# One-column products of the first feed-forward weights, spread between the steps of the output projection's last tile

## The chip, the cores and the metric

One Trainium2 chip, one of its cores. The metric is the device time of one execution in microseconds (us); lower is better. A core has five engines that run their own instruction streams and wait for each other through semaphores: TensorE (PE; its weight loads are shown apart as PEld), VectorE (DVE), ScalarE (ACT), GpSimd (POOL) and SyncE (SP), which issues most of the transfers.

## What is computed

Two transformer blocks run one after the other on 512 tokens of width 1024. The part that matters here is the end of the first block's token mixer and the start of its feed-forward network:

```python
x = x + g1 * token_mixer(...)                    # its last step: merged @ w_out
x = x + g2 * conv_ffn(ada_norm(x, norm2_g, sh2, sc2), p)

def ada_norm(x, g, shift, scale):
    return rmsnorm(x, g) * (1 + scale) + shift

def conv_ffn(h, p):
    u, g = jnp.split(h @ p['ffn_w_up'], 2, axis=-1)
    ...
```

The norm's input to `ffn_w_up` is a scaled x, divided by the root of a token's mean square, plus a shift that is the same for every token. So `h @ w` can be had from the raw, not yet divided x: (raw x @ w) / root + shift @ w. The kernel does this for the first pair of feed-forward tiles, and therefore needs `shift @ w` for those 2 x 128 columns: these are the one-column products that the change moves.

## The kernel before, in words

**Layout and precision.** Activations lie transposed: 128 channels on the partitions, eight tiles of channels, 512 tokens along the free axis. Each weight matrix comes in chunks of (mostly) 8 x 256 columns. SyncE loads a chunk into one of three staging buffers (WS), ScalarE writes its high part (WH, `hi_chunk`, line 88) and VectorE the rest (WL, `lo_chunk`, line 92). A product of a chunk with an activation is three matmuls per channel tile: high x high, high x low, low x high (`prod`, lines 477 to 479), so a tile of 128 outputs x 512 tokens takes 8 steps (k) of 3 matmuls. `prod_by_rows` (lines 498 to 500) does two output tiles at once, one channel tile after the other, and waits for each channel tile as it becomes ready.

**The output projection** (`out1_pe`) has 4 chunks and 8 output tiles n. Tile 7 is computed in PSUM bank 7; tile 6 in bank 0. VectorE (`out1_dve`) adds tile n to x (key "out1", n), sums squares and makes the low part of the raw scaled x; ScalarE squares and makes its high part. At the head of each chunk i both engines first convert a later chunk (OUT1+i+1, for i = 3 this is UP1, the first chunk of the feed-forward network).

**In the last tile**, TensorE runs six of the eight steps, then `shifted_pe`: for two groups of 128 columns, eight matmuls of 128 x 128 staged weights (float32, straight from WS) with one column of the shift, into bank 0, columns 0 and 1. Before them it waits for the low part of chunk UP1 and for VectorE having read bank 0 ("out1", 6). The last one signals "shifted". Then come the sums of seven squares over the channels (`seven_pe`, line 508), and then the last two steps of the tile. A float32 matmul shows in the trace as two passes, so the 16 products are 32 records of line 1602, and the four matmuls of line 508 are 8 records.

**Who waits for what.** SyncE waits for "shifted" before it loads chunk UP1+3 into the staging buffer of UP1 (line 397). VectorE waits for it before it copies the two columns out of bank 0 (line 1647), after the norm's diagonal. `up_pe` starts right behind `out1_pe` with the raw product of chunk UP1 (`prod_by_rows`); after two of its steps it adds the eighth square's sums (`eighth_pe`), from which ScalarE and VectorE get the norm; chunk UP1+1 then needs the normed x, and chunk UP1+2 is converted by VectorE after the last normed tile.

**Where to look:** the call is at line 1584 in `out1_pe`, `shifted_pe` at lines 1595 to 1604, `seven_pe` above line 508, the waits of the other engines at lines 397 and 1647. `modv_pe` (line 1419), two float32 matmuls with one column each, is a like piece of work in the same part of the kernel. The order on each engine is the order of the code; there is no scheduler.

Of the kernel before, what the change touches and what calls it, by code (L numbers as in the profile page):

```python
# [13 lines left out]
L = 512  # L14
# [117 lines left out]
def build(nc, A, out):  # L132
# [8 lines left out]
    def bank(b, n=512, p0=0, p1=128, off=0):  # L141
        return PS[p0:p1, b * 512 + off:b * 512 + off + n]

    pe, dve, acts, pool = (Tally(nc.alloc_semaphore(n)) for n in ("pe_done", "dve_done", "act_done", "pool_done"))
# [166 lines left out]
    def modcol(part, k, j=0):  # L311
        return MT[:, 8 * part + k, j:j + 1]
# [28 lines left out]
    UP1 = len(chunks)  # L341
# [31 lines left out]
    def stage(j):  # L373
        nk, n = chunks[j][1:3]
        return WS[:, slot(j), 0:nk * n]

    def weights(j):
        nk, n = chunks[j][1:3]
        return tuple(w[:, place(j), 0:nk * n].rearrange("p (k n) -> p k n", k=nk) for w in (WH, WL))
# [86 lines left out]
    def terms(w, wl, c, n=128, tok=(0, L), XX=(XHT, XLT), nk=8, k0=0):  # L466
        return [(w[:, k, c:c + n], wl[:, k, c:c + n], XX[0][:, k0 + k, tok[0]:tok[1]],
                 XX[1][:, k0 + k, tok[0]:tok[1]]) for k in range(nk)]
# [4 lines left out]
    def prod(e, o, trms, key=None, first=True, last=True):  # L473

        n = len(trms)
        for i, (lh, ll, rh, rl) in enumerate(trms):
            e.matmul(o, lh, rh, start=first and i == 0, stop=False)  # L477
            e.matmul(o, lh, rl, start=False, stop=False)  # L478
            ins = e.matmul(o, ll, rh, start=False, stop=last and i == n - 1)  # L479
        if key:  # L480
            ins.then_inc(*pe.to(*key))
# [7 lines left out]
    def prod_by_rows(e, outs, trms, ready, key, between={}):  # L489


        for k in range(8):
            if k in between:
                between[k]()
            e.wait_ge(*ready(k))
            for o, tm in zip(outs, trms):
                lh, ll, rh, rl = tm[k]
                e.matmul(o, lh, rh, start=k == 0, stop=False)  # L498
                e.matmul(o, lh, rl, start=False, stop=False)  # L499
                ins = e.matmul(o, ll, rh, start=False, stop=k == 7)  # L500
        ins.then_inc(*pe.to(*key))
# [3 lines left out]
    def sums_pe(e, name, tile, n, start, stop, key, step=512):  # L505
        for i, x in enumerate(range(0, n, 128)):
            w = min(128, n - x)
            ins = e.matmul(bank(3, 1, p1=w, off=step * i), tile[:, x:x + w], ONE[:, 0:1], start=start, stop=stop)
        ins.then_inc(*pe.to(*key))

    def spread_pe(e, name, n):

        e.wait_ge(*dve.at(name, "diagonal"))
        w = min(128, n)
        e.matmul(bank(3, n), ONE[0:w, :], RST[0:w, 0:n], start=True, stop=True).then_inc(*pe.to(name, "spread"))
# [4 lines left out]
    def seven_pe(e, name, n):  # L520
        e.wait_ge(*dve.at(name, "sum", 6))
        sums_pe(e, name, T[2], n, True, False, (name, "sums", 6))
# [893 lines left out]
    def modv_pe(e, i):  # L1416
        e.wait_ge(*dve.at("mod_half", i, 1))
        for m in range(2):
            ins = e.matmul(bank(7, 1, off=m), MACC[:, 128 * m:128 * m + 128], ONE[:, 0:1], start=True, stop=True)
        ins.then_inc(*pe.to("mod_sum", i))  # L1420
# [139 lines left out]
    def out1_bank(n):  # L1560
        return bank((1, 7, 2, 0, 1, 2, 0, 7)[n])

    def out1_pe(e):
        for i in range(4):
            j = OUT1 + i
            w, wl = weights(j)
            e.wait_ge(*dve.at("wl", j))
            tm = [terms(w, wl, 128 * m, XX=(MGH, MGL)) for m in range(2)]
            if i == 0:
                e.wait_ge(*dve.at("branch", 57))  # L1570
                prod_by_rows(e, [out1_bank(0), out1_bank(1)], tm, lambda k: dve.at("mg_lo", k), ("out1", 1))
            else:
                for m in range(2):
                    n = 2 * i + m
                    if n < 4:
                        e.wait_ge(*dve.at("branch", 56 + n if n == 2 else 63))
                    else:
                        e.wait_ge(*dve.at("out1", n - 3 if n > 4 else 1))
                    if n < 7:
                        prod(e, out1_bank(n), tm[m], ("out1", n))  # L1580
                    else:
                        e.wait_ge(*dve.at("mod", 23))
                        prod(e, out1_bank(n), tm[m][:6], last=False)
                        shifted_pe(e)
                        seven_pe(e, "norm2", L)
                        prod(e, out1_bank(n), tm[m][6:], ("out1", n), first=False)
            pe.name("w", j)
            if i == 2:
                e.wait_ge(*dve.at("meta_rms"))
            if i == 1:  # L1590
                spread_pe(e, "meta", 16)
                e.wait_ge(*dve.at("out1", 1))
                modv_pe(e, 23)

    def shifted_pe(e):

        e.wait_ge(*dve.at("wl", UP1))
        e.wait_ge(*dve.at("out1", 6))
        w = stage(UP1).rearrange("p (k n) -> p k n", k=8)
        for m in range(2):  # L1600
            for k in range(8):
                ins = e.matmul(bank(0, 1, off=m), w[:, k, 128 * m:128 * m + 128], modcol(3, k), start=k == 0,
                               stop=k == 7)
        ins.then_inc(*pe.to("shifted"))

    def out1_act(a):
        for i in range(4):
# [976 lines left out]
    def tensor(e):  # L2584
        front_pe(e)
        proj_pe(e)
        mix_pe(e)
        na_pe(e)
        gate_pe(e)
        out1_pe(e)  # L2590
        up_pe(e, "up1", UP1, "norm2", True)
        down_pe(e, "down1", "up1", DN1)
        foxp_pe(e)
        fox_pe(e)
        out2_pe(e)
        up_pe(e, "up2", UP2, "norm4", False)
        down_pe(e, "down2", "up2", DN2, "norm5")
        mean_pe(e, "norm5", L)
# [274 lines left out]
```

## Time and profile before

| | |
|---|---|
| median of 3 runs | 1680.36 us |
| lowest, highest | 1675.89 us, 1681.28 us |
| the profiled execution: span, first to last instruction | 1680.7 us |
| the profiled execution's own time outside the span | not given |
| TensorE busy | 1640.0 us, 98% |
| VectorE busy | 919.1 us, 55% |
| ScalarE busy | 632.4 us, 38% |
| mean granted TensorE clock | 0.988 of full |

All durations come from the one profiled execution. The ends of matmuls are modelled and overlap the next ones, so for TensorE the starts are read, not the durations: consecutive starts of 512-column matmuls lie 0.22 to 0.23 us apart.

### The profile page before, as it was taken

What the parts mean: (1) busy time and instruction counts of PE and PEld (TensorE: products, weight loads), DVE (VectorE), ACT (ScalarE), POOL (GpSimd) and SP (SyncE); (2) the same over time, 40 slices, a digit from 0 to 9 for tenths busy, and PEclk for the clock granted to TensorE, in tenths of its full rate; (3) what the DMA queues carried; (4) which work ended last, traced back from release to release, by engine and by line L of the source; (5) the groups of instructions that cost most, each with busy time, mean ns of one, the idle gap of its engine ahead of it and who ended that gap; (6) DMA issues with size and microseconds to landing.
All of it is one profiled execution on the core that took longest, in us unless ns stands there. A gap on an engine that the chain in (4) does not pass through costs nothing.

```text
span 1680.7 us, 20208 instructions
## 1 busy us (share of the span) xinstructions
PE 1640.0 (98%) x7941; PEld 1333.0 (79%) x7941; DVE 919.1 (55%) x1262; ACT 632.4 (38%) x816; POOL 92.6 (6%) x130
## 2 busy tenths in 40 slices
PE   8999999999999999999999999999999999999997
PEld 3588777878887888888888789977768888888885
DVE  5665686677667654444444574145766544444323
ACT  2352458432233343333332533146653332223221
POOL 0100000111010000000000100003420000000000
PEclk9899999999999999999999999999999999999998
DMA  9432101755444233332234221224442333332331
GB/s 320 129 119 80 44 26 51 226 164 179 160 150 151 64 102 85 101 101 77 86 103 131 86 76 52 76 65 96 97 127 75 101 100 101 100 90 66 92 104 51
DMA packets 227365, 176.71 MB, mean 105 GB/s; under 512 B 15812, under 2 KB 213316, under 8 KB 227270
## 3 DMA queue, kind: packets, MB, share of 16 engines
q1 hardware_dynamic: 220662, 151.23, 30.9%
q0 software_dynamic: 6608, 24.19, 4.4%
q8 instruction: 63, 1.03, 0.3%
q14 instruction: 32, 0.26, 0.0%
HBM read 166.84 MB, written 2.13 MB: 101 GB/s over the span
## 4 chain that ended last, share of the span: by engine, by line
PE 83%; DVE 9%; ACT 4%; issue 1%; SPq 1%; DMA 1%; DVEq 0%; POOLq 0%; POOL 0%; ACTq 0%
PE PS L477 23%; PE PS L479 23%; PE PS L478 23%; PE PS L2393 2%; PE PS L486 1%; DVE WL L92 1%; DVE T L92 1%; DMA MODW<-in_w_mod 1%; PE PS L498 1%; PE PS L500 1%; PE PS L499 1%; SPq L2682 1%; PE PS L649 1%; ACT WH L88 1%; DVE SUMS L111 1%
## 5 line engine op out<-in xcount | busy, mean ns | idle before, releaser
L477 PE MATMUL PS<-XH,WH 128*128 128x512 f32 (+2 forms) x1264 | 481.1, 381 | 3.2 <-DVE WL L92 1.1
L478 PE MATMUL PS<-XL,WH 128*128 128x512 f32 (+2 forms) x1264 | 476.8, 377 | 0.0
L479 PE MATMUL PS<-XH,WL 128*128 128x512 f32 (+2 forms) x1264 | 476.8, 377 | 0.0
L92 DVE TENSOR_TENSOR WL<-WS,WH 128x2048 fp32r<-128x2048 f32 (+3 forms) x131 | 272.8, 2083 | 209.4 <-ACT WH L88 206.6
L477 PEld LDWEIGHTS PS<-XH,WH 128*128 128x128 f32 (+1 forms) x1264 | 236.0, 187 | 48.9 <-DVE WL L92 2.0
L479 PEld LDWEIGHTS PS<-XH,WL 128*128 128x128 f32 (+1 forms) x1264 | 235.9, 187 | 44.8
L478 PEld LDWEIGHTS PS<-XL,WH 128*128 128x128 f32 (+1 forms) x1264 | 236.0, 187 | 43.2 <-issue 0.7
L88 ACT ACTIVATE WH<-WS 128x2048 fp32r<-128x2048 f32 (+3 forms) x131 | 229.1, 1749 | 76.2 <-PE PS L479 46.7
L477 PE MATMUL PS<-HH,WH 128*128 128x512 f32 x352 | 137.2, 390 | 0.2 <-DVE WL L92 0.2
L478 PE MATMUL PS<-HL,WH 128*128 128x512 f32 x352 | 136.9, 389 | 0.0
L479 PE MATMUL PS<-HH,WL 128*128 128x512 f32 x352 | 136.9, 389 | 0.0
L88 ACT ACTIVATE T<-T 128x512 f32<-128x512 f32 x45 | 28.5, 632 | 172.4 <-DVE T L92 138.8
L477 PEld LDWEIGHTS PS<-HH,WH 128*128 128x128 f32 x352 | 66.1, 188 | 14.3 <-DVE WL L92 0.6
L478 PEld LDWEIGHTS PS<-HL,WH 128*128 128x128 f32 x352 | 66.1, 188 | 13.8
L479 PEld LDWEIGHTS PS<-HH,WL 128*128 128x128 f32 x352 | 66.1, 188 | 13.6
L92 DVE TENSOR_TENSOR T<-PS,RST 128x512 f32<-128x512 f32 x47 | 32.5, 692 | 78.3 <-PE PS L479 69.2
L103 DVE SCALAR_TENSOR_TENSOR T<-PS,VT,T 128x511 f32<-128x511 f32 x42 | 31.5, 750 | 54.7 <-ACT T L88 53.9
L88 ACT ACTIVATE T<-X 128x512 f32<-128x512 f32 x40 | 25.3, 632 | 90.4 <-DVE X L92 58.9
L103 DVE SCALAR_TENSOR_TENSOR MACC<-MSRC,CACT,MACC 128x256 f32<-128x256 f32 x112 | 54.3, 485 | 8.3 <-DMA MSRC<-in_w_mod 3.6
L477 PE MATMUL PS<-WH,XH 128*128 128x256 f32 (+1 forms) x192 | 54.4, 283 | 0.0
L478 PE MATMUL PS<-WL,XH 128*128 128x256 f32 (+1 forms) x192 | 53.8, 280 | 0.0
L479 PE MATMUL PS<-WH,XL 128*128 128x256 f32 (+1 forms) x192 | 53.7, 280 | 0.0
(373 smaller groups left out, 2294.7 us busy)
## 6 DMA issues: line engine op xcount, KB each, us to landing
WS<-in_w_in SPq DMA_DIRECT2D x24, 1024.0 KB, 5.4
WS<-in_ffn_w_up SPq DMA_DIRECT2D x44, 512.0 KB, 4.9
WS<-in_ffn_w_in SPq DMA_DIRECT2D x44, 512.0 KB, 4.8
MSRC<-in_w_mod POOLq DMA_DIRECT2D x32, 512.0 KB, 4.9
WS<-in_fox_w_in SPq DMA_DIRECT2D x16, 1024.0 KB, 5.6
WS<-in_ffn_w_down SPq DMA_DIRECT2D x16, 704.0 KB, 4.5
WS<-in_ffn_w_out SPq DMA_DIRECT2D x16, 704.0 KB, 4.5
MODW<-in_w_mod SPq DMA_DIRECT2D x8, 1024.0 KB, 11.7
```

Source lines behind the costliest of these rows:

```text
L88: self.e.activation(o, i, f, scale=scale, **kw).then_inc(*self.done.to(*key))
L92: self.e.tensor_tensor(o, a, b, op).then_inc(*self.done.to(*key))
L103: self.e.scalar_tensor_tensor(o, a, s, b, op0, op1).then_inc(*self.done.to(*key))
L111: self.e.reciprocal(o, a).then_inc(*self.done.to(*key))
L477: e.matmul(o, lh, rh, start=first and i == 0, stop=False)
L478: e.matmul(o, lh, rl, start=False, stop=False)
L479: ins = e.matmul(o, ll, rh, start=False, stop=last and i == n - 1)
L486: ins = e.matmul(o, l, r, start=i == 0, stop=i == n - 1)
L498: e.matmul(o, lh, rh, start=k == 0, stop=False)
L499: e.matmul(o, lh, rl, start=False, stop=False)
L500: ins = e.matmul(o, ll, rh, start=False, stop=k == 7)
L2393: ins = e.matmul(PS[:, b + q0:b + L], VP[h % 2][0:k, t, :], P[h % 2][0:k, PFROM[t]:PFROM[t] + L - q0], start=t == 0, stop=t == 4)
```

## The change

The last tile's eight steps are run one by one. After each of the steps 1 to 6, TensorE computes 3, 3, 2, 3, 3 and 2 of the 16 one-column products (6, 6, 4, 6, 6 and 4 passes); after step 6 come the sums of seven squares, then step 7. The waits for the low part of UP1 and for "out1", 6 stand before the first one-column product, so after step 1 instead of after step 5. The products themselves, their banks and their results are the same.

```diff
--- before.py
+++ after.py
@@ -1580,10 +1580,13 @@
                         prod(e, out1_bank(n), tm[m], ("out1", n))
                     else:
                         e.wait_ge(*dve.at("mod", 23))
-                        prod(e, out1_bank(n), tm[m][:6], last=False)
-                        shifted_pe(e)
-                        seven_pe(e, "norm2", L)
-                        prod(e, out1_bank(n), tm[m][6:], ("out1", n), first=False)
+                        for k in range(8):
+                            prod(e, out1_bank(n), tm[m][k:k + 1], ("out1", n) if k == 7 else None, first=k == 0, last=k == 7)
+                            if 1 <= k < 7:
+                                for p in range(*((0, 3), (3, 6), (6, 8), (8, 11), (11, 14), (14, 16))[k - 1]):
+                                    shifted_pe(e, *divmod(p, 8))
+                            if k == 6:
+                                seven_pe(e, "norm2", L)
             pe.name("w", j)
             if i == 2:
                 e.wait_ge(*dve.at("meta_rms"))
@@ -1592,16 +1595,15 @@
                 e.wait_ge(*dve.at("out1", 1))
                 modv_pe(e, 23)
 
-    def shifted_pe(e):
-
-        e.wait_ge(*dve.at("wl", UP1))
-        e.wait_ge(*dve.at("out1", 6))
+    def shifted_pe(e, m, k):
+
+        if m + k == 0:
+            e.wait_ge(*dve.at("wl", UP1))
+            e.wait_ge(*dve.at("out1", 6))
         w = stage(UP1).rearrange("p (k n) -> p k n", k=8)
-        for m in range(2):
-            for k in range(8):
-                ins = e.matmul(bank(0, 1, off=m), w[:, k, 128 * m:128 * m + 128], modcol(3, k), start=k == 0,
-                               stop=k == 7)
-        ins.then_inc(*pe.to("shifted"))
+        ins = e.matmul(bank(0, 1, off=m), w[:, k, 128 * m:128 * m + 128], modcol(3, k), start=k == 0, stop=k == 7)
+        if m + k == 8:
+            ins.then_inc(*pe.to("shifted"))
 
     def out1_act(a):
         for i in range(4):
```

## Rows read from the trace of the kernel before

**Rows 1.** The page: span, and TensorE's busy time.

```profile
span 1680.7 us, 20208 instructions
...
PE 1640.0 (98%) x7941; PEld 1333.0 (79%) x7941; DVE 919.1 (55%) x1262; ACT 632.4 (38%) x816; POOL 92.6 (6%) x130
```

**Rows 2.** The page: chain that ended last, shares by engine and line.

```profile
PE PS L477 23%; PE PS L479 23%; PE PS L478 23%; PE PS L2393 2%; PE PS L486 1%; DVE WL L92 1%; DVE T L92 1%; DMA MODW<-in_w_mod 1%; PE PS L498 1%; PE PS L500 1%; PE PS L499 1%; SPq L2682 1%; PE PS L649 1%; ACT WH L88 1%; DVE SUMS L111 1%
```

**Rows 3.** Busy time by stretch: engines, PEclk the granted clock, DMA.

```profile
core 0: us, PE busy (x) PEld busy (x) DVE busy (x) ACT busy (x) POOL busy (x), PEclk, DMA share, GB/s
...
550.00:554.00 4.00, 4.00 (x32) 3.73 (x30) 1.44 (x2) 1.55 (x3) 0.00 (x0) 0.98 0.00 0
554.00:557.60 3.60, 3.60 (x18) 3.60 (x19) 0.00 (x0) 0.00 (x0) 0.00 (x0) 0.50 0.05 13
...
560.70:564.00 3.30, 3.30 (x20) 2.83 (x18) 1.35 (x2) 1.36 (x2) 0.00 (x0) 1.00 0.05 11
```

**Rows 4.** Timeline of TensorE: start us, us, engine line op out<-in xcount.

```profile
548.72 0.39 PE L477 MATMUL PS<-MGH,WH 128*128 128x512 f32 x1
...
551.44 4.59 PE L1602 MATMUL PS<-MODT,WS 128*128 128x1 f32 x32
555.89 1.84 PE L508 MATMUL PS<-ONE,T 128*128 128x1 f32 x8
557.60 0.77 PE L477 MATMUL PS<-MGH,WH 128*128 128x512 f32 x1
...
560.30 0.58 PE L498 MATMUL PS<-GXH,WH 128*128 128x512 f32 x1
560.72 0.39 PE L499 MATMUL PS<-GXL,WH 128*128 128x512 f32 x1
```

**Rows 5.** Chain of waits in order of time: start us, us, what.

```profile
563.39 0.80 PE PS L508 x8
...
564.59 1.93 ACT WH L88
...
582.63 2.30 DVE WL L92
...
584.98 0.50 PE PS L477
```

**Rows 6.** Timeline of VectorE, end of the output projection.

```profile
546.81 2.29 DVE L92 TENSOR_TENSOR WL<-WS,WH 128x2048 fp32r<-128x2048 f32 x1 [1.24 <-ACT WH L88]
549.21 0.75 DVE L103 SCALAR_TENSOR_TENSOR X<-PS,MODT,X 128x512 f32<-128x512 f32 x1
550.65 0.69 DVE L92 TENSOR_TENSOR T<-T,T 128x512 f32<-128x512 f32 x1 [0.70 <-ACT T L88]
```

**Rows 7.** Timeline of TensorE, eight one-column passes at full clock.

```profile
563.23 0.95 PE L508 MATMUL PS<-ONE,T 128*128 128x1 f32 x8
564.04 0.49 PE L498 MATMUL PS<-GXH,WH 128*128 128x512 f32 x1
564.36 0.40 PE L499 MATMUL PS<-GXL,WH 128*128 128x512 f32 x1
```

**Rows 8.** Timeline, VectorE and TensorE: four one-column passes behind a wait.

```profile
529.74 0.75 DVE L103 SCALAR_TENSOR_TENSOR X<-PS,MODT,X 128x512 f32<-128x512 f32 x1
...
530.46 0.61 PE L1419 MATMUL PS<-ONE,MACC 128*128 128x1 f32 x4
...
530.93 0.48 PE L477 MATMUL PS<-MGH,WH 128*128 128x512 f32 x1
```

**Rows 9.** Timeline of ScalarE: high part of chunk UP1+3.

```profile
587.28 1.92 ACT L88 ACTIVATE WH<-WS 128x2048 fp32r<-128x2048 f32 x1
```

**Rows 10.** Busy time by stretch elsewhere, columns as in rows 3.

```profile
203.00:207.00 4.00, 1.66 (x9) 1.10 (x8) 3.13 (x5) 3.75 (x4) 0.00 (x0) 1.00 0.00 0
...
1192.00:1195.60 3.60, 2.01 (x9) 1.24 (x8) 3.26 (x5) 0.59 (x1) 0.62 (x2) 1.00 0.89 204
1195.60:1199.00 3.40, 3.40 (x18) 3.20 (x16) 2.82 (x7) 0.00 (x0) 0.00 (x0) 0.50 0.29 75
```

## The prediction

> **What bounds the kernel now.** I read the page's head first: TensorE is busy for 98% of the span [rows 1], and the chain that ended last runs through its lines [rows 2]. So a change of TensorE's order counts wherever the chain is on TensorE, and other engines count only where they make it wait. Next, the granted clock by stretch around the edited call. In 550 to 554 it is 0.98, in 554 to 557.6 it is 0.50, and from 560.7 on it is 1.00 again [rows 3]: the two levels are 2.4 and 1.2 GHz. What TensorE did before the fall is in its timeline: from 551.44 it had only the 32 passes of line 1602, one column each, behind a stretch of 512-column matmuls [rows 4]. It was never idle there (busy 4.00 of 4.00) [rows 3], yet it came down to the half clock, and the rest of the passes, the sums and the last six matmuls ran at it.
>
> The chain then shows what hangs on the end of this tile: the last sums at 563.39, ScalarE's weights at 564.59, VectorE's normed tiles and weights up to 582.63, and TensorE again at 584.98 [rows 5]. All of it starts from the end of tile 7, so what this tile gains or loses passes on whole to 584.98 and, TensorE being the bound behind it, to the end.
>
> **The sum, step by step.** It is a difference of starts in one execution. That execution's span is 1680.7 us [rows 1]; what lies around the span is not given, and the median of the three runs is 0.3 us under the span, so I carry the difference to the median, 1680.36.
>
> *Price of a pass at full clock.* Eight passes behind a 512-column matmul start at 563.23, the next matmul at 564.04 and the one after it at 564.36 [rows 7]. Ordinary matmuls lie 0.227 apart: twelve between 548.72 and 551.44 take 2.72 [rows 4]. So the group costs 0.81, and 0.32 - 0.23 = 0.09 for the return to long matmuls, 0.90 together. Four passes that stood behind a wait take 530.46 to 530.93, 0.47 [rows 8], with the same 0.09 0.56; here the first weight load has nothing to hide behind. If that load costs as much as a pass, 8 passes are 0.90 and 5 are 0.56: 0.113 each, and a boundary costs nothing beyond it.
>
> *Removed: the half clock.* At full clock the 40 passes and six matmuls from 551.44 would take 40 x 0.113 + 6 x 0.227 = 5.88 and end at 557.32. The feed-forward product starts at 560.30 instead, and its first matmul takes 0.42 (to 560.72) where 0.23 is normal [rows 4]. That is 2.98 + 0.19 = 3.17 us lost. If the clock holds with the passes spread, all of it comes back: **-3.17**.
>
> *Added: a wait that was hidden.* "out1", 6 and the low part of UP1 are now awaited after step 1. Step 2 starts at 548.72 [rows 4], which is where the first pass would go. VectorE finishes the low part at 546.81 + 2.29 = 549.10 and only then runs the addition of tile 6, 549.21 + 0.75 = 549.96 [rows 6]. Neither moves: both follow ScalarE's conversion and tile 6, which are ahead of the edit. In a like wait TensorE started 0.03 before VectorE's recorded end, 530.46 against 529.74 + 0.75 = 530.49 [rows 8], so it goes on at 549.93. That is 1.21 of idle, and 0.11 for the weight load that now hides behind nothing: **+1.32**. Before, this wait was over long before 551.44. Its bounds are 0 (if VectorE is early) and 1.5. Behind the waiting product stand all further matmuls of the tile, and no other engine needs any of them before the tile's end.
>
> *Five more boundaries.* The passes stand in six groups instead of one (the last with the sums). By the equations above a boundary is worth 0. The bounds are one weight load of 0.11 gained or lost at each of five, -0.6 and +0.6; I take 0, because rows 7 is exactly such a group, hidden load, exposed return and all.
> The Trainium skill, TensorE: Matmul & The Clock Gate, Part 2 (Step-by-step), says that the queue pulls a weight load ahead of running matmuls. By that alone the spread would hide five more loads, 0.6 us, for 1677.9; the row shows that the matmul behind the group pays it back [rows 7].
>
> *Moved at no cost.* The sums of seven squares wait for 550.65 + 0.69 = 551.34 [rows 6] and now start near 557, so they don't wait. "shifted" comes near 557.0 instead of 555.9: the load of chunk UP1+3 is queued behind it on SyncE, about 1 us later, and ScalarE wants that chunk only at 587.28 [rows 9]. VectorE copies the two columns only after the norm's diagonal, which follows the sums at 563.39 [rows 5]. POOL has nothing here. If the first of these covers went, a late chunk would stop TensorE at its fourth pair of tiles, but 25 us lie between.
>
> Sum: -3.17 + 1.32 + 0 = -1.85. The feed-forward product should start at 548.72 + 1.32 + 40 x 0.113 + 6 x 0.68 = 558.64 instead of 560.30. 1680.36 - 1.85 = **1678.5 us**, 0.11% less. About 0.3%, here 5.0 us, is what a measurement of this kernel can tell from no change; the whole forecast lies inside it.
>
> **The rivals.**
>
> *The clock falls all the same (slower than before).* Place: the first group. The new wait leaves TensorE idle for 1.2 us, and the groups behind it are still half one-column passes. For it: two other falls have idle time just ahead, 2.01 busy of 3.60 before the 0.50 at 1195.6 [rows 10]. Against it: 1.66 busy of 4.00 at 203 to 207 left the clock at 1.00 [rows 10], and between the new groups stand 0.68 us of full matmuls. Before, there was nothing of the kind from 551.44 to the fall, which a mean of 0.98 over 550 to 554 [rows 3] puts near 553.85. Price: with the same 3.17 lost, only the wait is left, +1.32, 1681.7. It decides for slower as soon as the clock is down for more than 1.85 / 0.5 = 3.7 us; at half clock through all of the 8.6 us of work it would be 8.6 + 1.3 - 3.2 = +6.7, 1687.1.
> The Trainium skill, TensorE: Matmul & The Clock Gate, Part 1 (HAM oscillation), warns of long idle gaps between bursts of matmuls, and the same part says that the gate goes by how busy TensorE has been. Taken at its word it speaks against this change, which adds a gap and removes none; its time would be this rival's 1681.7. The trace disagrees in part: TensorE was busy without a gap and lost its clock [rows 3].
>
> *No wait shows.* If VectorE's order gives bank 0 earlier than the rows say, the whole 3.17 comes back: 1677.2. Against it stand two VectorE instructions in a row that end at 549.96 [rows 6].
>
> *It changes nothing to be seen.* If the fall of the clock comes in only some executions, or a later fall (the one at 1195.6 lasts 3.40 us [rows 10], which cost 1.7) comes or goes as everything shifts by 2 us, the difference may be nothing, 1680.4, or 1678.5 - 1.7 = 1676.8. For it: the three runs lie 5.4 us apart, more than the whole sum. Against it: the passes that brought the fall stand in the code and are the same in every execution.
>
> **How the numbers follow.** Forecast 0.60. Clock falls all the same 0.15, nearly all of it within 5 us of before. No wait shows 0.08. Nothing to be seen, or a later fall moved, 0.17. The range reaches down to 1675.0 (1676.8, and below it the 1.8 us that two medians of such runs may well differ by) and up to 1682.0, past the rival's 1681.7; up to 2 in 10 lie outside. Faster by over 0.3% needs 1675.3 or less: 0.10, from the last case's low end. Slower by over 0.3% needs 1685.4: 0.03, from a long half clock. Within: 0.87.
>
> **What would show it.** In the new profile: PEclk 1.00 from 548 to 564 (the rival: 0.50 somewhere in it); a gap in TensorE's timeline of about 1.2 us from 548.7, ended by VectorE's X; groups of 6, 6, 4, 6, 6 and 12 passes at 0.11 each with three matmuls between them; the first matmul of line 498 near 558.6; the last part of the chain before the feed-forward tiles (584.98 before) near 583.1; the chunk UP1+3 on time. The forecast is wrong if the clock is at half in that stretch, if the gap is missing or twice as long, or if the stretch gains its 1.85 us and the total doesn't.

## The result, and the profile after

The change made the kernel slower: a median of 1687.3 us over 22 runs (1674.7 to 1692.1) against 1680.7 over 22 runs of the kernel before (1675.6 to 1687.8), a ratio of 1.0033 with a 95% interval of [1.0018, 1.0048]. The forecast was 1678.5.

The two profiled executions hide this: their spans are 1680.4 us after and 1680.7 before. What tells them apart is the granted clock. By stretch, in the kernel after (columns: stretch, its length, busy time of PE, PEld, DVE, ACT, POOL with instruction counts, PEclk, DMA share, GB/s):

```profile
541.60:545.50 3.90, 2.67 (x15) 2.04 (x15) 3.10 (x3) 1.20 (x2) 0.00 (x0) 1.00 0.00 0
545.50:558.30 12.80, 12.80 (x49) 11.45 (x48) 0.88 (x2) 0.36 (x2) 0.00 (x0) 0.50 0.01 4
558.30:562.60 4.30, 4.30 (x11) 3.43 (x12) 1.19 (x2) 1.35 (x2) 0.00 (x0) 0.50 0.84 232
562.60:566.00 3.40, 3.40 (x20) 2.94 (x20) 1.12 (x3) 1.09 (x2) 0.00 (x0) 1.00 0.00 0
48.70:62.40 13.70, 12.48 (x29) 4.93 (x28) 11.80 (x19) 7.34 (x10) 3.37 (x3) 1.00 0.02 5
```

The clock falls at 545.5, 1.1 us behind the first of the moved passes (544.38), and stays at 1.2 GHz for 17.1 us, until 562.6. Before, the fall near the tile lasted from about 553.9 to 560.7, 6.8 us [rows 3]. The last row is luck, since the code there is the same in both kernels: in this execution the clock was full from 48.7 to 62.4, whereas in that of the kernel before it was at half (with the first matmul of its tile 7):

```profile
48.70:62.40 13.70, 12.87 (x15) 4.76 (x16) 8.61 (x14) 5.52 (x7) 3.36 (x3) 0.50 0.02 7
...
547.36 0.39 PE L477 MATMUL PS<-MGH,WH 128*128 128x512 f32 x1
```

So tile 7 begins at 541.64 instead of 547.36, 5.7 us earlier, before the change has done anything, and the change then gives it all back. TensorE's timeline after shows how:

```profile
542.77 0.39 PE L479 MATMUL PS<-MGH,WL 128*128 128x512 f32 x1
544.38 0.80 PE L1604 MATMUL PS<-MODT,WS 128*128 128x1 f32 x6 [1.23 <-DVE X L103]
545.05 0.48 PE L477 MATMUL PS<-MGH,WH 128*128 128x512 f32 x1
...
546.07 1.27 PE L1604 MATMUL PS<-MODT,WS 128*128 128x1 f32 x6
547.21 0.77 PE L477 MATMUL PS<-MGH,WH 128*128 128x512 f32 x1
...
555.89 0.85 PE L1604 MATMUL PS<-MODT,WS 128*128 128x1 f32 x4
556.59 1.85 PE L508 MATMUL PS<-ONE,T 128*128 128x1 f32 x8
558.30 0.77 PE L477 MATMUL PS<-MGH,WH 128*128 128x512 f32 x1
...
559.73 0.63 PE L498 MATMUL PS<-GXH,WH 128*128 128x512 f32 x1
```

Between the last matmul of step 1 and the first pass lie 1.61 us where 0.23 is normal: 1.38 of idle, ended by VectorE's addition of tile 6. The first group of six passes takes 0.67 (544.38 to 545.05), the second 1.14 (546.07 to 547.21), and a step of three long matmuls 1.42 instead of 0.68. From the start of tile 7 to the feed-forward product (line 498) it takes 559.73 - 541.64 = 18.09 us, before 560.30 - 547.36 = 12.94. The clock is back only at 562.6, after 4.3 us of long matmuls without passes. The long fall is probably not in every execution: two of the 22 took 1674.7 and 1674.9 us with a mean clock of 0.993, which is about 23 us at half clock in all, where the profiled one had 36. No trace of those two shows it.

Behind this the chain is as before and only later, so the loss passes on whole (chain of waits after; the answers of [rows 5]):

```profile
563.98 0.80 PE PS L508 x8
...
565.18 1.93 ACT WH L88
...
583.20 2.30 DVE WL L92
...
585.55 0.50 PE PS L477
```

From the start of tile 7 to here it is 43.9 us after and 37.6 before. The chunk UP1+3 was on time (ScalarE's timeline after, [rows 9]):

```profile
587.85 1.92 ACT L88 ACTIVATE WH<-WS 128x2048 fp32r<-128x2048 f32 x1
```

One execution of the experiment e4 below took 2728 us at a mean granted clock of 0.555; it was slow as a whole and is left out of e4's figures.

### The profile page after: what moved, and what is told of

The parts are those of the page before. It is cut to its first block, busy times and chain, and to the rows that moved or that the text cites. A ratio compares the mean times of both kernels' runs of the same rounds, so it can differ in the third digit from the quotient of the medians.

```text
span 1680.4 us, 20208 instructions
## 1 busy us (share of the span) xinstructions
PE 1639.0 (98%) x7941; PEld 1333.5 (79%) x7941; DVE 917.4 (55%) x1262; ACT 632.4 (38%) x816; POOL 92.3 (5%) x130
## 4 chain that ended last, share of the span: by engine, by line
PE 81%; DVE 11%; ACT 4%; issue 2%; DMA 1%; DVEq 0%; SPq 0%; POOLq 0%; POOL 0%; ACTq 0%
PE PS L477 23%; PE PS L479 23%; PE PS L478 22%; PE PS L2395 2%; DVE WL L92 2%; PE PS L486 1%; DVE T L92 1%; PE PS L614 1%; ACT WH L88 1%; PE PS L498 1%; PE PS L500 1%; PE PS L499 1%; DVE SUMS L111 1%; ACT NTP L88 1%; ACT T L88 1%
## 5 line engine op out<-in xcount | busy, mean ns | idle before, releaser
L92 DVE TENSOR_TENSOR T<-PS,RST 128x512 f32<-128x512 f32 x47 | 32.5, 691 | 78.3 <-PE PS L479 69.2
```

The source lines that it names most:

```text
L92: self.e.tensor_tensor(o, a, b, op).then_inc(*self.done.to(*key))
```

## The experiments

Two parts can be told apart: the wait that was moved ahead (idle time), and the spread of the passes. The first theory was that the spread mix brings the clock down and holds it down; its rival was that the idle time does. Both were wrong, and a third, that it takes the two together, was stated for the second set. All kernels below were timed in 12 runs each (e4 counts 11), beside the kernel before (29 to 35 runs, medians 1679.6, 1679.9 and 1680.1).

"Half clock" in the table is the time at half clock per execution, 2 x (1 - mean granted clock) x span, averaged over the runs; the clock of each run is given to 0.001, so a single run is good to 1.7 us only. The runs of one kernel scatter by about 10 us in it, so a mean of 12 runs is good to about 3 us. "At the tile" is the granted clock of the profiled execution from the start of tile 7 to the feed-forward product.

| kernel | median us | ratio to before, 95% | half clock, us | at the tile |
|---|---|---|---|---|
| before | 1679.6 to 1680.1 | 1 | 35.0, 36.6, 39.4 | 0.75 |
| the change, 22 runs | 1687.3 | 1.0033 [1.0018, 1.0048] | 49.7 | 0.61 |
| f1, the change again | 1686.6 | 1.0044 [1.0026, 1.0061] | 49.4 | 0.61 |
| e1, wait alone | 1679.7 | 1.0003 [0.9982, 1.0024] | 32.5 | 0.95 |
| e2, spread, no wait | 1676.1 | 0.9983 [0.9961, 1.0004] | 27.9 | 1.00 |
| f3, as e2, wait put back | 1685.3 | 1.0028 [1.0009, 1.0047] | 45.2 | 0.61 |
| f2, spread late | 1672.9 | 0.9973 [0.9953, 0.9993] | 24.6 | 1.00 |
| g2, f2 again | 1675.2 | 0.9965 [0.9943, 0.9987] | 27.4 | 1.00 |
| f4, wait early, spread late | 1678.4 | 0.9996 [0.9980, 1.0012] | 31.6 | 0.94 |
| g1, wait, then all together | 1683.4 | 1.0016 [0.9996, 1.0035] | 38.4 | 0.77 |
| g3, the change, half the products | 1675.7 | 0.9976 [0.9955, 0.9997] | 30.4 | 1.00 |
| e3, one or two a step, tiles 6 and 7 | 1675.8 | 0.9971 [0.9954, 0.9987] | 25.1 | 1.00 |
| e4, 15 of 16 products left out | 1676.6 | 0.9977 [0.9957, 0.9996] | 36.2 | 1.00 |

### e1: the wait alone

```diff
...
-                        prod(e, out1_bank(n), tm[m][:6], last=False)
+                        prod(e, out1_bank(n), tm[m][:2], last=False)
+                        e.wait_ge(*dve.at("wl", UP1))
+                        e.wait_ge(*dve.at("out1", 6))
+                        prod(e, out1_bank(n), tm[m][2:6], first=False, last=False)
                         shifted_pe(e)
```

> The 16 products stay together behind step 5 as before; only the two waits stand behind step 1. Theory 'mix' (short passes spread between long matmuls bring the clock down and keep it down; the wait is only its own idle time): at most the wait's 1.3 us over the kernel before, so a median of 1680 to 1684 and half clock of 3 to 10 us around the last tile. Theory 'wait' (the idle time ahead of the passes makes the clock fall and the rest follows): as slow as the change, 1685 to 1690, with half clock for over 10 us in that stretch.

```profile
541.60:553.60 12.00, 10.79 (x66) 9.26 (x66) 3.97 (x4) 1.56 (x3) 0.00 (x0) 0.95 0.12 33
552.50:555.90 3.40, 3.40 (x10) 2.65 (x9) 0.75 (x1) 1.25 (x2) 0.00 (x0) 0.50 0.98 276
```

No loss that can be measured, 1679.7. The same 1.2 us of idle is there (10.79 busy of 12.00), and the clock did not fall behind it. It fell only at 552.5, 0.9 us into the long matmuls behind the passes and the sums (they start at 551.59), and for 3.4 us, where the kernel before lost it in the middle of the passes and for 6.8. That does not make the wait free: over the runs there are 2.5 us less at half clock (32.5 against 35.0), within the scatter, and that much would be worth 1.25 of its 1.5 us. The theory that the idle time alone brings the loss is out.

### e2: the spread without the wait

```diff
-            e.wait_ge(*dve.at("wl", UP1))
-            e.wait_ge(*dve.at("out1", 6))
+            e.wait_ge(*acts.at("wh", UP1))
...
-        ins = e.matmul(bank(0, 1, off=m), w[:, k, 128 * m:128 * m + 128], ...
+        ins = e.matmul(bank(6, 1, off=8 + m), w[:, k, 128 * m:128 * m + 128], ...
...
```

> The change's order, but the products go to two free columns of bank 6 and wait only for ScalarE's high part of the chunk, so that no idle time stands behind step 1. Theory 'mix': the clock falls as with the change and stays at half until the dense matmuls are back, 1684 to 1690, about 1.3 us under the change. Theory 'wait': clock 1.00 through the tile, 1677 to 1680, under the kernel before.

```profile
542.30:552.30 10.00, 10.00 (x66) 8.99 (x65) 3.92 (x4) 1.56 (x3) 0.00 (x0) 1.00 0.02 3
```

1676.1, not over 1684: the mix of passes and long matmuls alone held the full clock, though half of the time of a step is passes (six at 0.113 beside three long matmuls at 0.227). It is also a little under the 1677 to 1680 of the other theory; the interval of its ratio touches 1. The theory that the mix brings the clock down by itself is out too. The tile took 10.00 us; the forecast's price list (24 matmuls of 0.227 and 40 passes of 0.113) gives 9.97.

### e3: a thinner mix over two tiles

Bank 6 as in e2; one product behind each step of tile 6 and 2, 1, 2, 1, 1, 1 behind steps 0 to 5 of tile 7, waiting only for the chunk to arrive:

```diff
+            e.wait_ge(ws_in[slot(UP1)], arrived[UP1])
...
+                    elif n == 6:
+                        for k in range(8):
+                            prod(e, out1_bank(n), tm[m][k:k + 1], ("out1", n) if k == 7 else None, first=k == 0, last=k == 7)
+                            shifted_pe(e, 0, k)
...
```

> One or two products (2 or 4 passes) a step, over tiles 6 and 7, into bank 6, waiting only for the chunk's arrival; no idle time, and the short passes are a quarter of TensorE's time where the change has a half. Theory 'mix': a thin mix holds the clock, so it stays at 1.00 but for a possible fall at the sums, 1676 to 1680. Theory 'wait': the same, 1677 to 1680; a rival that any one-column pass lets the clock fall gives over 1684.

```profile
537.90:551.80 13.90, 13.90 (x81) 12.10 (x80) 5.93 (x6) 4.62 (x6) 0.00 (x0) 1.00 0.13 34
```

The stretch shown begins in step 2 of tile 6. 1675.8, below before with its whole interval and as good as e2. Both theories had said very nearly this (1676 or 1677 to 1680), so it parted nothing.

### e4: 15 of the 16 products left out

```diff
-        for m in range(2):
-            for k in range(8):
+        for m in range(1, 2):
+            for k in range(7, 8):
...
```

> The kernel before with only the last of the 16 one-column products left, the other 15 left out, so the feed-forward network's first pair lacks its shift. If the loss of the kernel before is the 30 passes (3.4 us at full clock) and their half clock (3.2 us), this is 4 to 7 us under before, 1674 to 1677, with no half clock at the tile, though the falls early in the program stay. It bounds what any placement of the products can reach: before minus 3.2 us.

```profile
551.10:557.60 6.50, 6.50 (x35) 5.58 (x34) 3.91 (x4) 1.56 (x3) 0.00 (x0) 1.00 0.12 33
```

1676.6, at the edge of what was expected. In its profile the tile went through in 6.6 us at full clock, but in the mean over its runs the kernel spent 36.2 us at half clock, no less than before (35.0). The missing 30 passes are 3.4 us, and the means over the runs differ by 3.5 (1675.8 against 1679.3), so nothing of the half clock's 3.2 is seen back. Whether the clock fell elsewhere in those runs or at the tile after all isn't shown. So the bound that it was meant to give is blurred, and it came out no faster than kernels that do all the products.

### f1: the change again

> The change itself, measured again beside the others. The wait alone gave 1679.7 us against 1679.6 for before, the spread alone 1676.1. If the loss is real and comes from the two together: 1684 to 1690 again, and a stretch of over 10 us at half clock around the last tile. If the first measurement was an odd set of executions: 1676 to 1681, between the two single edits, and no such stretch.

```profile
545.90:563.90 18.00, 16.76 (x66) 14.59 (x64) 3.92 (x4) 1.56 (x3) 0.00 (x0) 0.61 0.09 25
563.90:566.90 3.00, 3.00 (x9) 2.32 (x8) 1.31 (x2) 1.35 (x2) 0.00 (x0) 0.50 0.71 199
```

The loss is real, 1686.6, and the tile again takes 18.0 us with the clock down to 566.9.

### f2 and g2: the spread, late enough that nothing waits

```diff
-                            if 1 <= k < 7:
-                                for p in range(*((0, 3), (3, 6), (6, 8), (8, 11), (11, 14), (14, 16))[k - 1]):
+                            if 3 <= k < 7:
+                                for p in range(4 * k - 12, 4 * k - 8):
```

> Bank 0 and the change's two waits, but the products come behind steps 3 to 6, four at a time, when both waits are over, so no idle time. Theory 'together' (idle time right ahead of the thin mix lets the clock fall, and the mix, at half clock, keeps it down): clock mostly 1.00, 1675 to 1679, like the spread without a wait. Theory 'groups' (larger groups are what hurts; eight passes a step are more than half the time): 1683 or more.

```profile
541.60:551.70 10.10, 10.10 (x65) 8.89 (x64) 3.98 (x4) 1.55 (x3) 0.00 (x0) 1.00 0.02 5
```

The bank and the waits of the change, only without idle time, and the kernel is faster than before, and under the 1675 to 1679 expected. Groups of eight passes, more than half of each step's time, don't hurt. Measured a second time:

> The best kernel so far, again: products behind steps 3 to 6, four at a time, bank 0, the change's waits. 1672.9 was measured, against 1676.1 for the spread behind steps 1 to 6 without a wait. If the gain over the kernel before is real, 1671 to 1677 and a ratio below 1 with its whole interval.

```profile
545.70:555.80 10.10, 10.10 (x66) 8.92 (x65) 3.95 (x4) 1.56 (x3) 0.00 (x0) 1.00 0.01 3
```

Again below before with its whole interval: 0.9965 [0.9943, 0.9987]. This is the change as it should have been placed, 1672.9 and 1675.2 us. Not all of the 6.9 and 4.8 us between the medians is shown to be the tile's doing: 12.94 to 10.08 us there, and 0.19 behind it, give 3.1. The time at half clock is 12 us less than before in both sets (24.6 against 36.6, 27.4 against 39.4) where the fall at the tile is 6.8 us; part of that can be scatter.

### f3: e2 with the wait put back

e2's bank 6, but the two waits of the change in place of the one on ScalarE.

> The change with the products in bank 6 and both of its waits kept: it differs from the spread without a wait (1676.1) by the idle time alone. Theory 'together': as slow as the change, 1684 to 1690. Theory 'bank' (bank 0 was what made the difference): 1677 to 1679, the 1.3 us of idle over the spread without a wait.

```profile
541.60:559.80 18.20, 16.97 (x66) 14.71 (x65) 3.97 (x4) 1.55 (x3) 0.00 (x0) 0.61 0.09 26
```

One edit, the idle time, moves e2's 1676.1 to 1685.3 and e2's 10.0 us of tile to 18.1. The two were timed in different sets, but their ratios to the kernel before, timed beside each, have intervals that lie apart (to 1.0004, and from 1.0009). The bank has no part in it.

### f4: the idle time early, the spread late

The waits stand behind step 1 as in the change, the products behind steps 3 to 6 as in f2.

> The idle time stays behind step 1, but two full steps (1.4 us of long matmuls) stand between it and the first products, which come four at a time behind steps 3 to 6. Theory 'together', strictly (idle and mix have to touch): 1677 to 1681. If it is enough that both fall in the same few us, it stays slow, 1683 to 1690.

```profile
542.20:554.30 12.10, 10.87 (x65) 9.38 (x64) 3.97 (x4) 1.56 (x3) 0.00 (x0) 0.94 0.06 15
```

1678.4: the long fall is avoided. The clock did fall in this profile, but only at 552.9, where the sums end, and for 3.4 us. f4 differs from the change in two things, the two dense steps (long matmuls without passes) between the idle time and the passes, and the grouping by eight; since the same groups alone are harmless (f2), the distance is the likelier reason, but no run has the change's own groups at that distance.

### g1: the wait, then all products at once

```diff
...
-                        prod(e, out1_bank(n), tm[m][:6], last=False)
+                        prod(e, out1_bank(n), tm[m][:2], last=False)
                         shifted_pe(e)
+                        prod(e, out1_bank(n), tm[m][2:6], first=False, last=False)
...
```

> Both waits behind step 1 as in the change, but all 16 products follow at once (32 passes), and steps 2 to 5 come dense behind them. The change has three things: idle time, the passes right behind it, and then 9 us in which passes and long matmuls alternate. If the alternation is what keeps the clock at half once it has fallen: it falls here too but is back within the dense steps, 3 to 10 us at half clock, 1679 to 1684. If idle time and passes touching is what costs, however they are arranged afterwards: over 10 us at half clock, 1684 to 1690.

```profile
541.70:546.10 4.40, 3.17 (x22) 2.58 (x21) 3.50 (x4) 1.55 (x3) 0.00 (x0) 1.00 0.00 0
546.10:552.90 6.80, 6.80 (x26) 6.22 (x26) 0.49 (x1) 0.00 (x0) 0.00 (x0) 0.50 0.22 59
552.90:556.40 3.50, 3.50 (x21) 2.99 (x21) 0.00 (x0) 0.00 (x0) 0.00 (x0) 1.00 0.68 185
```

The idle time and the passes touch here as in the change, and the clock falls near the same place, 1.6 us behind the first pass (1.1 in the change). But the long matmuls behind them are dense, starting at 549.88:

```profile
544.49 5.53 PE L1603 MATMUL PS<-MODT,WS 128*128 128x1 f32 x32 [1.23 <-DVE X L103]
549.88 0.77 PE L477 MATMUL PS<-MGH,WH 128*128 128x512 f32 x1
```

and 3.0 us later, at 552.9, the clock is back: 6.8 us at half instead of 17.1. The median, 1683.4, lies between before and the change; its interval still touches 1, so the size of its loss is not settled. Over the runs the time at half clock is that of the kernel before (38.4 against 39.4 us), and the means over the runs, 1682.2 against 1680.6, differ by no more than the wait.

### g3: the change with half of the products

Channel tiles 0 to 3 are left out of the shift's products, so 2, 1, 1, 2, 1 and 1 products stand behind steps 1 to 6, and the wait and its idle time are the change's.

> The change with half of the products left out (channel tiles 0 to 3), so the shift is summed over half of its channels: 1 or 2 products a step behind steps 1 to 6, the waits behind step 1 as in the change. If the share of one-column passes behind the idle time decides, a quarter instead of a half lets the clock stay or come back soon: 1675 to 1680, under 10 us at half clock. If any alternation holds it down: 1682 or more, 15 us or more at half clock.

```profile
541.80:551.50 9.70, 8.47 (x49) 7.12 (x49) 3.99 (x4) 1.56 (x3) 0.00 (x0) 1.00 0.03 7
```

With half of the passes behind the same idle time the clock held in the profile, the tile took 9.68 us, and the runs are below before with their whole interval (1675.7 us). So it is not any mix behind idle time that brings the long fall; how thick it has to be isn't shown. This also gives the price of the wait at full clock: 24 matmuls and 24 passes by the price list are 8.16, so the wait costs 1.52.

## Why the prediction was wrong

**The step that failed** is "If the clock holds with the passes spread, all of it comes back: -3.17". It didn't hold. At full clock the tile with its wait would take e2's 10.00 and 1.52 for the wait, 11.52; it took 18.09, so 6.57 were lost to the half clock, and another 1.34 in the first seven feed-forward matmuls (559.73 to 562.66, 2.93 us where 7 x 0.227 is 1.59). That is 7.91 lost where 3.17 was to be won back. With the wait: -3.17 + 7.91 + 1.52 = +6.26 us; the stretch from the start of tile 7 to the chain's next TensorE matmul is 6.3 longer, and the medians differ by 6.6. The size of the term was right: where the clock held, in e2, the tile took 10.00 instead of 12.94, and with the 0.19 behind it that is 3.13. What was wrong is that the spread would hold the clock behind the new wait.

**The rival was the right one and was given 0.15.** "The clock falls all the same" named the place (the first group, behind the new idle time) and the point from which it decides (3.7 us at half clock); its likeliest price, a fall as long as before, was too low, and the 17.1 us measured lie near its other end, at half clock through all of the tile. That this end's 1687.1 meets the median of 1687.3 so closely is in part luck: it counts nothing behind the tile, and takes half clock as exactly twice the time. What the prediction didn't see is that the alternation of passes and long matmuls, once the clock is down, doesn't bring it up again. At full clock the same alternation holds it (e2, f2, g2), and dense matmuls bring it back in both g1 (3.0 us of them) and the change (4.3 us). The prediction took the length of the fall from the kernel before [rows 3], where dense matmuls stood right behind the passes; that choice was the error, more than the chance.

The row that the prediction held against this rival was one execution's: 1.66 busy of 4.00 at 203 to 207 left the clock at 1.00 [rows 10]. In the profile of e4, whose code is the same up to there and whose TensorE was busy for 2.01 of that stretch, the clock fell right behind it (the kernel before, then e4):

```profile
206.80:213.70 6.90, 6.45 (x30) 5.73 (x31) 6.39 (x7) 1.39 (x3) 0.00 (x0) 1.00 0.18 54
206.80:213.70 6.90, 6.11 (x15) 4.90 (x16) 4.35 (x4) 1.13 (x2) 0.00 (x0) 0.51 0.13 35
```

It fell there in f1 and g2 too. A place where the clock held in one profile is no sign that it holds in the next.

**The idle gap.** The Trainium skill, TensorE: Matmul & The Clock Gate, Part 1 (HAM oscillation), warns of long idle gaps, and the prediction counted it against the change. The trace agrees with it in half: without the gap nothing was lost (e2), but the gap of 1.38 us alone cost its own time only (e1); gap and passes side by side cost 7.9 us (the change; f3's tile is as long).

**The wait** was sized at +1.32 and measured 1.52 (g3). The idle is 1.38 instead of 1.21, since TensorE started 0.14 after VectorE's recorded end and not 0.03 before it:

```profile
543.49 0.75 DVE L103 SCALAR_TENSOR_TENSOR X<-PS,MODT,X 128x512 f32<-128x512 f32 x1
```

543.49 + 0.75 = 544.24, and the first pass starts at 544.38.

**The boundaries** were taken at 0 between -0.6 and +0.6, and that was right: 10.00 in e2 and 10.08 in f2 against 9.97. The 0.6 us that the prediction worked out from the weight loads pulled ahead, as the Trainium skill, TensorE: Matmul & The Clock Gate, Part 2 (Step-by-step), tells of them, do not appear.

**What was moved at no cost** had none: the sums follow the last products without a gap, and UP1+3 was converted at 587.85, in its turn behind the chain.

**The range**, up to 1682.0, left out the outcome because its upper end took the rival at its likeliest price and not at its bound of 1687.1, which was worked out and then not used.

Still open is why idle time and passes have to touch, and how many passes it takes (g3 had half and held). The runs show the combinations that fall (idle then passes, in f3, g1 and the change) and those that hold, each in one or two profiled executions and in the mean half-clock time of their runs; they don't show what the chip measures.

## What to carry to other kernels

Before moving a piece of short matmuls to an earlier place, look at what it waits for there: a wait that was hidden becomes idle time, and idle time right ahead of a run in which one-column passes and long matmuls alternate can cost far more than itself (here 7.9 us lost to half clock, beside 1.5 for the wait). Spread such passes where nothing waits (behind step 3 here, not step 1), and keep a stretch of long matmuls right behind any place where the clock may fall, since nothing else brought it back here. When times scatter by several us with the clock, compare the mean time at half clock over many runs: one profiled execution of each kernel would have shown no change here.

## What the runs showed of the hardware that was not expected

A mix in which half of TensorE's time is one-column passes held 2.4 GHz when it was entered at full clock (e2, f2, g2), and the change's mix stayed at 1.2 GHz for 12.8 us without recovering. Idle time of 1.4 us, which alone cost only itself (e1), decides between the two (e2 and f3).

The falls elsewhere in the program come and go between executions of the same code: one at 48.7 to 62.4 was in the profile before and not in the one after, which is 5.7 us of start for the tile. A fall at 201 to 214 was in the profiles of e4, f1 and g2 and in no other. Such falls are a good part of the 12 us by which runs of one kernel differ.
